# Gate rows of the chunked DeltaNet layer: four transposes of gate columns in place of four products, and the decay behind the post-norm

## The reference

```python
beta = jax.nn.sigmoid(b)
g = -jnp.exp(a_log) * jax.nn.softplus(a + dt_bias)
...
G = jnp.cumsum(gc, axis=-1)
decay = jnp.exp(jnp.where(causal, G[..., :, None] - G[..., None, :], -jnp.inf))
...
lower = jnp.where(strict, jnp.einsum('bhnid,bhnjd->bhnij', k_beta, kc) * decay, 0.0)
...
attn_intra = jnp.einsum('bhnid,bhnjd->bhnij', qc, kc) * decay
q_exp = qc * jnp.exp(G)[..., None]
k_tail = kc * jnp.exp(G[..., -1:] - G)[..., None]
g_last = jnp.exp(G[..., -1])
...
y = jnp.einsum('bse,ed->bsd', jnp.concatenate([o_a, o_b], axis=-1), w_out[l])
x = x + rmsnorm(y, post_norm_w[l])
```

## Time and profile before

| | |
|---|---|
| median of three runs | 2417.44 us |
| lowest, highest | 2415.66, 2420.44 us |
| the profiled execution's own time | 2413.75 us |
| its span, first to last instruction | 2411.9 us |
| PE busy | 2212.0 us (92%) |
| PE weight loads busy | 1893.9 us (79%) |
| DVE busy | 1689.2 us (70%) |
| ACT busy | 780.6 us (32%) |
| POOL busy | 652.8 us (27%) |
| mean granted TensorE clock | 0.992 of full speed |
| chain that ended last | PE 79%, DVE 11%, issue 6%, ACT 2%, DMA 1% |

### The profile page before, as it was taken

The page is one execution under the profiler, slowest core; times in us unless marked ns, Lnnn a source line. Parts: engine busy times, 40 slices in busy tenths (PEclk is TensorE's granted clock), DMA queues, the critical chain, the costliest instruction groups (busy, mean ns, idle before and its releaser), DMA issues.

```text
span 2411.9 us, 63703 instructions
## 1 busy us (share of the span) xinstructions
PE 2212.0 (92%) x25926; PEld 1893.9 (79%) x25926; DVE 1689.2 (70%) x4495; ACT 780.6 (32%) x2008; POOL 652.8 (27%) x875
## 2 busy tenths in 40 slices
PE   0489999999999999999999999999999999999996
PEld 0488878878888888888888887888888888888884
DVE  5887667767676676767677677676767677676764
ACT  0533333333333332333333333333333333233332
POOL 0022222322232323222223223232323232322322
PEclk9999999999999999999999999999999999999998
DMA  7000000000000000000000000000000000000000
GB/s 305 27 20 29 29 3 29 29 29 29 29 29 3 29 29 30 29 30 1 29 29 29 30 29 16 15 29 30 29 29 29 2 29 29 30 29 29 11 10 27
DMA packets 26363, 75.76 MB, mean 31 GB/s; under 512 B 5129, under 2 KB 9538, under 8 KB 25026
## 3 DMA queue, kind: packets, MB, share of 16 engines
q1 hardware_dynamic: 26050, 71.29, 8.5%
HBM read 54.50 MB, written 16.78 MB: 30 GB/s over the span
## 4 chain that ended last, share of the span: by engine, by line
PE 79%; DVE 11%; issue 6%; ACT 2%; DMA 1%; SPq 0%; POOL 0%; DVEq 0%; POOLq 0%; ACTq 0%
PE bank L408 29%; PE bank L600 11%; PE bank L415 10%; PE bank L423 9%; DVE qkv L873 4%; PE bank L458 3%; PE bank L438 3%; PE bank L568 2%; PE bank L534 2%; DVE w_raw L1209 1%; PE bank L555 1%; PE bank L386 1%; PE bank L442 1%; PE bank L446 1%; DVE small L912 1%
## 5 line engine op out<-in xcount | busy, mean ns | idle before, releaser
L408 PE MATMUL bank<-xt_half,w_raw 128*128 128x128 f16 x15360 | 933.9, 220 | 54.8 <-DVE w_raw L1209 54.3
L408 PEld LDWEIGHTS bank<-xt_half,w_raw 128*128 128x128 f16 x15360 | 896.8, 98 | 62.3 <-DVE w_raw L1209 54.6
L873 DVE SCALAR_TENSOR_TENSOR qkv<-conv_in,cols,qkv 128x128 f32<-128x128 f32 x1152 | 439.1, 423 | 4.0
L415 PE MATMUL bank<-w_raw,xt_half 128*128 128x264 f16 (+1 forms) x1536 | 283.0, 328 | 0.0
L1266 POOL TENSOR_TENSOR cw<-mt,small 128x256 f32<-128x256 f32 x160 | 114.5, 723 | 401.2 <-PE bank L438 377.6
L415 PEld LDWEIGHTS bank<-w_raw,xt_half 128*128 128x128 f16 x1536 | 147.9, 98 | 77.7 <-issue 5.3
L665 ACT ACTIVATE tanh_c<-qkv 128x512 f32<-128x512 f32 x96 | 60.5, 630 | 373.7 <-DVE qkv L873 373.7
L600 PE MATMUL bank<-w_o,inv_t 128*128 128x512 f16 x768 | 172.7, 382 | 2.1 <-DVE inv_t L1145 2.1
L700 ACT ACTIVATE work<-bank 128x256 f32<-128x256 f32 x160 | 60.7, 380 | 346.0 <-PE bank L442 346.0
L600 PE MATMUL bank<-w_o,out_b_half 128*128 128x512 f16 x768 | 171.0, 379 | 0.0
L458 PE MATMUL bank<-work 128*128 128x128 f32 x640 | 101.5, 281 | 56.0 <-ACT work L700 55.1
(11 more groups left out here) (219 smaller groups left out, 3849.3 us busy)
## 6 DMA issues: line engine op xcount, KB each, us to landing
x_in<-in_x_dram SPq DMA_DIRECT2D x32, 512.0 KB, 3.7
y_out<-in_x_dram SPq DMA_DIRECT2D x32, 512.0 KB, 4.2
out_dram<-y_out SPq DMA_DIRECT2D x32, 512.0 KB, 2.9
w_raw<-in_w_in_dram SPq DMA_DIRECT2D x8, 1024.0 KB, 12.6
w_o<-in_w_out_dram SPq DMA_DIRECT2D x8, 512.0 KB, 13.0
w_raw<-in_w_in_dram SPq DMA_DIRECT2D x8, 384.0 KB, 11.7
w_raw<-in_w_in_dram SPq DMA_DIRECT2D x8, 256.0 KB, 12.5
rot_tab<-in_rotary_dram SPq DMA_DIRECT2D x32, 64.0 KB, 3.4
```

The source lines that it names most:

```text
L408: last = mm(dst[:, 128 * b:128 * b + 128], w_half[:, c, ws, col:col + 128], xt_half[:, xs, c, :], start=(c == 0 and ws + xs == 0), stop=(c ...
L415: last = mm(dst[:, 0:n_col], xt_half[:, xs, c, :], w_half[:, c, ws, col:col + n_col], start=(c == 0 and ws + xs == 0), stop=(c == NC - 1 a ...
L873: last = v.scalar_tensor_tensor(dst, conv_in[:, b, i:i + TOK], tap, dst, ALU.mult, ALU.add)
```

## The change

On PE the four products into `bank[2]` go. The column product now leads the step. After k and v are turned and one piece is filled, PE waits for `g_cols_used` and `state_ready`, and transposes the four columns of `g_cols`, each broadcast over the array; then two pieces are filled, as part of the three that stood there. On DVE the columns are copied first, then `finish(m - 1)` runs, and only then the last column is copied, the difference formed and the decay's argument computed. The new event `g_last_ready` links the copy with the difference.

```diff
--- before.py
+++ after.py
@@ -215,6 +215,7 @@
             sem(n) for n in ("kv_raw_ready", "k_rot_ready", "q_raw_ready", "q_rot_ready", "ab_ready"))
         gate_link, soft_arg_ready, soft_exp_ready, g_ready = (
             sem(n) for n in ("gate_link", "soft_arg_ready", "soft_exp_ready", "g_ready"))
+        g_last_ready = sem("g_last_ready")
         g_col_t, g_row_t, g_cols_used, decay_arg_ready, decay_ready, exp_cols_ready = (
             sem(n) for n in ("g_col_t", "g_row_t", "g_cols_used", "decay_arg_ready", "decay_ready",
                              "exp_cols_ready"))
@@ -472,11 +473,6 @@
                     return
 
                 done(pe, g_ready, m)
-                done(pe, state_ready, m - 1)
-                for h in range(4):
-                    last = mm(bank[2][:, 128 * h:128 * h + 128], g_tok[:, h:h + 1].broadcast_to([128, 128]),
-                              upper, start=True, stop=True)
-                last.then_inc(g_row_t, 1)
                 done(pe, out_a_ready, m - 1)
                 mm(bank[3][:, 0:4], upper, g_tok, start=True, stop=True).then_inc(g_col_t, 1)
                 done(pe, qkv_ready[1], m)
@@ -490,7 +486,13 @@
                 for h in range(4):
                     last = nc.tensor.transpose(heads(7)[:, h, :], v4[:, h, :], ident)
                 last.then_inc(v_turned, 1)
-                fill(3)
+                fill(1)
+                done(pe, g_cols_used, m)
+                done(pe, state_ready, m - 1)
+                for h in range(4):
+                    last = nc.tensor.transpose(heads(2)[:, h, :], g_cols[:, h:h + 1].broadcast_to([128, 128]), ident)
+                last.then_inc(g_row_t, 1)
+                fill(2)
 
                 done(pe, y_used, m - 1)
                 per_head(4, k4, k4, gram_t)
@@ -962,25 +964,24 @@
                 gate_steps = gates(t) if proj else None
                 if mix:
 
-                    done(dve, g_row_t, m)
                     done(dve, exp_cols_ready, m - 1)
-                    v.tensor_copy(g_cols[:, 8:12], heads(2)[:, :, TOK - 1])
                     done(dve, g_col_t, m)
                     v.tensor_copy(g_cols[:, 0:4], bank[3][:, 0:4]).then_inc(g_cols_used, 1)
-                    done(dve, g_cols_used, m)
+                    if first:
+                        dve.wait_ge(pw_loaded, 16)
+                        v.tensor_scalar(post_w, post_w, D ** 0.5, None, ALU.mult).then_inc(post_w_ready, 1)
+                        dve.wait_ge(post_w_ready, 1)
+                    else:
+                        finish(m - 1)
+                    done(dve, g_row_t, m)
+                    v.tensor_copy(g_cols[:, 8:12], heads(2)[:, :, TOK - 1]).then_inc(g_last_ready, 1)
+                    done(dve, g_last_ready, m)
                     v.tensor_tensor(g_cols[:, 4:8], g_cols[:, 8:12], g_cols[:, 0:4], ALU.subtract)
                     done(dve, aw_ready, m - 1)
                     for h in range(4):
                         last = v.scalar_tensor_tensor(decay[:, h, :], heads(2)[:, h, :], g_cols[:, h:h + 1], neg,
                                                       ALU.subtract, ALU.add)
                     last.then_inc(decay_arg_ready, 1)
-                    if first:
-                        dve.wait_ge(pw_loaded, 16)
-                        v.tensor_scalar(post_w, post_w, D ** 0.5, None, ALU.mult).then_inc(post_w_ready, 1)
-                        dve.wait_ge(post_w_ready, 1)
-                    else:
-                        finish(m - 1)
-
                     done(dve, k_sq_ready, m)
                     v.tensor_reduce(norms[:, 0:4], prod, AX_X, ALU.add).then_inc(k_sq_used, 1)
                     done(dve, k_sq_used, m)
```

## The result

The changed kernel took 2434.08 us (median of four runs, 2433.20 to 2435.66); the kernel before, beside it, 2418.94 us (2415.66 to 2420.84). The ratio is 1.0058, with a 95% interval of 1.0041 to 1.0074: slower by 0.4 to 0.7%. The forecast was 2432 us, within 2419 to 2444. The profiled execution took 2434.74 us; that of before, with 2413.75 us, was among the quickest of its kernel (31 timed later took 2413.34 to 2423.42 us), so the two traces are 21 us apart where the medians are 15.

A forecast was written before the change was run, and what follows sets the result against it. TensorE, busy 92% of the span, was taken as the bound. The terms -7.5 + 6.4 + 10.2 + 7 + 1 gave +17.1 us on 2413.75, 2430.9; the forecast was 2432 us, 8 times in 10 within 2419 to 2444.

The forecast's parts named there:

- Straight starts: 17 tile starts in straight code: transposes cheaper than products, 0.44 us less each on TensorE, 7.5 us gained.
- Rival 4: Columns' copy too late in straight starts as well, gain gone (+8 us); 2446 us with all clock falls; chance 0.12.
- The wait at the edges: 13 loop edges: TensorE waits 2.9 us before the transposes, Gram products start 0.49 us later, 6.4 us lost.
- The clock: Behind the 13 loop edges: ten falls of TensorE's granted clock instead of four, 1.7 us each, 10.2 us lost.
- Rival 1: Clock falls no more often than before: +6.9 us, about 2422 to 2424 us; chance 0.17.
- The first tile: First mixing tile: VectorE's copy comes late, TensorE stops after one piece and turns q 5.1 us later; 7 us lost.
- Rival 2: First tile's loss hidden and no further clock falls: no change, 2414 to 2418 us; chance 0.08.
- The decay behind the post-norm: VectorE's copy, difference and decay moved behind the post-norm: cost zero in 31 tiles, up to 1 us in all.
- The two cases: Difference and decay either run beside GpSimd's addition, or are held until it ends, VectorE's start some 2.5 us later.
- The last tile: No projection hides the delayed decay there: 0 to 2.4 us lost, taken as 1.
- Rival 3: VectorE's idle time at loop edges shrinks: about 2410 us with a third less, 2378 if gone; chance 0.05.

The follow-up runs named there:

- e1: Kernel before the change with only VectorE's new order (columns' copy, post-norm, then decay), TensorE's list as before: 2393.44 us, ratio 0.9894 to the kernel before.
- e2: TensorE's list as after the change, VectorE's old order with the post-norm behind the decay: 2439.96 us, ratio 1.0090 to the kernel before.
- e4: Changed kernel with the four transposes behind the Gram products in the first mixing tile alone: 2431.23 us, ratio 1.0053 to the kernel before.
- e8: Changed kernel with the first input of the difference read from PSUM instead of its SBUF copy: 2428.51 us, only one run.
- e3: Changed kernel with TensorE computing the first projection piece twice more before its wait, in the loop's first step: 2417.37 us, ratio 0.9993 to the kernel before.
- e7: Changed kernel with four steps in the loop's body, so 6 loop edges instead of 13: 2389.36 us, ratio 0.9880 to the kernel before.
- e6: Changed kernel with the four transposes behind the Gram products: 2398.87 us, ratio 0.9915 to the kernel before.
- e5: Changed kernel with the four transposes behind all three projection pieces instead of the first: ratio 0.9889 to the kernel before, four runs of 2386.18 to 2393.03 us.
- e11: Like e9, but with all 33 steps written out instead of the hardware loop: 2362.52 us, ratio 0.9761 to the kernel before.
- e9: Changed kernel, transposes behind the third piece (first mixing tile: behind the Gram products), difference read from PSUM: 2380.38 us, ratio 0.9838 to the kernel before.

## Why the prediction was right, step by step

- **Straight starts:** 0.44 us less forecast, 0.45 measured; the 0.25 us of cover were 0.32, and no wait came. Rival 4 is out.
- **The wait at the edges:** forecast 2.9 to 3 us, ended by the columns' copy; measured 2.84 to 3.39 us at the 13 edges, 47.1 us over 15 waits. From VectorE's first instruction to the Gram products it is 3.39 us against 3.33 forecast; by the length of the tile an edge loses 0.50 us, where 0.49 was forecast. The prediction did not price the two halves of the change apart, though: e1 shows that this near-zero is a gain from VectorE's new order that TensorE's new order takes back.
- **The clock:** ten falls forecast, twelve found, three of them of twice the length, which I had not priced. The three other kernels with the same waits had 7 (e2), 12 (e4) and 10 (e8) of 13, so ten was the right size. This is the term that was mis-sized: in the traces it is 16.9 us more than before by the windows, or 15.6 by the lengths of the tiles, against 10.2 in the sum; even the bound of 15.3 for falls at all thirteen was too low, because of the long ones. Rival 1 (no further falls) is out. e3 shows the cause by itself: filling the wait takes the falls away. Part of the excess is the low base, which I had left open: the profiled execution of before had a mean granted clock of 0.992 and ran 5 us under its median, where the 31 executions timed beside the experiments had 0.987 to 0.993, median 0.990. The four of the changed kernel had 0.983 to 0.985, the traced one 0.985. How many falls an ordinary execution of before has was not traced. Whether the new transposes themselves count as work for the clock stays open too; no run tells it.
- **The first tile:** 7 us forecast. Q is turned 154.48 - 147.86 = 6.6 us after VectorE's copy, where it had been 0.3; 6.3 us. (It was to start near 156 us and started at 154.48, because the copy itself was 1.07 us early.) e4 gave 5.9 us of it back in the trace. Rival 2 is out.
- **The decay behind the post-norm:** nothing, as forecast. L987 (now L988) fell from 1.92 to 0.62 us in most tiles, because the decay now runs beside GpSimd's addition. The two cases that I had kept both occur: the difference got through in 29 tiles and was held for 2.35 us in tiles 30 to 32. The Trainium skill ("SBUF — State Buffer", "Who interferes with whom") says that a VectorE instruction with two inputs in SBUF contends with a GpSimd instruction that reads SBUF, and that the order of issue decides which of them blocks. The trace after agrees with the order (0.16 us when VectorE was first, 2.35 us when it was not), and e8 with the inputs.
- **The last tile:** 1 us forecast, 0.6 in the traces (60.55 to 61.10 us from VectorE's first instruction of the step to the end). That is luck in part: the mean granted clock of that tile was 0.87 before and 0.93 after. e8, without the hold, was 1.7 us shorter at 0.90, so the hold seems to cost at least that.
- **Rival 3** (VectorE's idle time shrinks) did not happen: 47.0 us at 13 edges after, 46.2 before. But e7 shows that it was not absurd: with a longer body in the loop it shrinks.

The sum was +17.1; the medians moved by 15.1 and the traces by 21. The traces' 21.0 us are: straight starts -7.8, the order at the edges +6.5, the clock there +15.6, the first tile +6.3, the last +0.6, VectorE's idle time at the jumps +0.8, and the setup before the first copy -1.1. So every step was there and of the right sign, and the step that was sized worst is the clock's. That the median came within 2 us of the forecast is partly luck: the clock's term was too small against the trace of before, and that trace was quicker than the ordinary execution of its kernel.

Still open: why with two steps in the body VectorE idles so long at the jump and no other engine comes near it, why less with four, and why ScalarE then idles as well. Which waits bring the clock down can't be told from their length alone: one of 3.29 us in e2 did not, one of 1.94 us in e6 did.

## What to carry to other kernels

Before an instruction with a wait is put into a list, look at what will be behind it. Here cheap transposes took two pieces of independent work out of a wait that another engine imposes 13 times, and lost nearly four times what they saved (28 us in the traces against 7.8); behind that work the same transposes cost nothing at the edges (e5 against e1: the tile is 67.55 us in both). Look at the wait where the other engine is latest (the loop's jump, the first tile), not where the timeline is typical. And price a longer idle time of TensorE with the clock that follows it.

## What the runs showed of the hardware

- 48 redundant products in a wait made the kernel 16.7 us faster (e3), by keeping the granted clock at 1.00.
- VectorE idled 3.5 us at each jump of a loop with two steps, 2.4 us with four, and not at all with the steps written out, with the same instructions. ScalarE did not with two steps and did for 1.0 to 1.3 us with four (e7); TensorE's weight loads waited at most 0.7 us there. Writing the loop out cost nothing that can be measured in 33 steps (e11).
- A VectorE instruction of 0.16 us with two inputs in SBUF took 2.35 us when GpSimd's addition had started 0.02 us earlier, and 0.16 us when that started 0.06 us later or when one input lay in PSUM (e8, e9).
- A stretch of the lower clock (1.2 GHz) followed four of TensorE's 13 waits at the edges before, of 1.99 to 2.10 us each, and none of the three longest, of 2.19 to 2.31 us; after waits of 2.7 to 3.4 us it came at 12, 7, 12 and 10 of 13 edges (the changed kernel, e2, e4, e8).
